# Odd layer: bias masked where it lands, and norm and stores between the products of the projection

## The reference, cut to what matters

```python
def natten_qkv(u, q_g, k_g):
    q, k, v = [t.reshape(B, T, NA_HEADS, NA_DIM) for t in jnp.split(u, 3, -1)]
    return rms_norm_2(q, q_g), rms_norm_2(k, k_g), v

def one_row(r):            # neighbourhood_attention, one row of 64 queries
    ...
    bias = jnp.transpose(rpb[:, drow][:, :, dcol], (0, 2, 1, 3))
    s_loc = einsum('bchd,bicjhd->bhcij', q_row, k_win) * scale + bias
    s_ctx = einsum('bchd,bnhd->bhcn', q_row, k_ctx) * scale
    p = softmax(concatenate([s_loc, s_ctx], -1))
    return p_loc @ v_win + p_ctx @ v_ctx
```

## Time and profile before

| | |
|---|---|
| runs of the kernel | 3016.82, 3017.26, 3021.13 us, median 3017.26 |
| span of the profiled execution | 3016.0 us |
| TensorE busy | 2677.4 us, 89% |
| VectorE busy | 1330.7 us, 44% |
| ScalarE busy | 490.4 us, 16% |
| GpSimd busy | 26.4 us, 1% |
| mean granted clock of TensorE | 0.955 |
| transfers | 651.34 MB, mean 216 GB/s |

### The profile page before, as it was taken

One profiled execution on the slowest core, in us unless ns is written; L12 is line 12 of the kernel. 1 busy time (PEld: TensorE's weight loads), 2 busy tenths in 40 slices (PEclk: granted clock), 3 DMA queues, 4 the chain that ended last, 5 costly groups with the idle time before them and its releaser, 6 DMA issues. The chain is left out here.

```text
span 3016.0 us, 44924 instructions
## 1 busy us (share of the span) xinstructions
PE 2677.4 (89%) x19748; PEld 1652.4 (55%) x19748; DVE 1330.7 (44%) x2509; ACT 490.4 (16%) x1158; POOL 26.4 (1%) x48
## 2 busy tenths in 40 slices
PE   7989999999999999998999989889979898865665
PEld 3467844446767888735753333345449687432323
DVE  2775488442473876586321111131367763100001
ACT  1023200000213000225221111020051311100000
POOL 0000000000000000000000000000000000000000
PEclk9999999999999999998999999999989999978878
DMA  9530255342352676220159999982110007899998
GB/s 358 195 140 26 87 195 223 139 168 112 112 195 71 251 279 248 75 84 29 59 232 402 427 428 428 427 339 46 44 36 30 2 25 301 366 427 428 427 427 353
DMA packets 67938, 651.34 MB, mean 216 GB/s; under 512 B 14880, under 2 KB 26912, under 8 KB 28064
## 3 DMA queue, kind: packets, MB, share of 16 engines
q1 hardware_dynamic: 67744, 648.47, 53.3%
HBM read 644.12 MB, written 4.33 MB: 215 GB/s over the span
## 5 line engine op out<-in xcount | busy, mean ns | idle before, releaser
L375 PE MATMUL ps<-HT,ring 128*128 128x256 f32 (+1 forms) x3152 | 901.3, 444 | 6.4 <-ACT HT L617 2.3
L375 PEld LDWEIGHTS ps<-HT,ring 128*128 128x128 f32 x3152 | 589.0, 190 | 284.5 <-issue 225.8
L2443 PE MATMUL ps<-ring,arena 128*32 128x256 f32 (+1 forms) x2944 | 372.9, 509 | 106.7 <-DMA ring<-in_moe_w 97.2
L477 DVE SCALAR_TENSOR_TENSOR acc<-ring,sil,acc 128x512 f32<-128x512 f32 x616 | 411.7, 744 | 0.0
L375 PE MATMUL ps<-arena,ring 128*128 128x256 f32 (+3 forms) x1232 | 373.6, 464 | 3.4 <-PEq L718 2.2
L2443 PEld LDWEIGHTS ps<-ring,arena 128*32 128x32 f32 (+1 forms) x2944 | 140.8, 131 | 315.0 <-issue 198.3
L375 PEld LDWEIGHTS ps<-arena,ring 128*128 128x128 f32 (+2 forms) x1232 | 230.1, 188 | 139.3 <-issue 119.3
L1042 DVE SCALAR_TENSOR_TENSOR XT<-ps,modcols,XT 128x256 f32<-128x256 f32 x124 | 55.7, 481 | 266.1 <-PE ps L375 140.4
L2464 PE MATMUL ps<-ring,arena 128*32 128x256 f32 x960 | 83.7, 510 | 58.6 <-DMA ring<-in_moe_w 58.6
L2464 PE MATMUL ps<-ring,conv 128*64 128x512 f32 x496 | 112.3, 596 | 24.0 <-DMA ring<-in_moe_w 23.3
L495 ACT ACTIVATE modrows<-ps 128x128 f32<-128x128 f32 x44 | 12.2, 278 | 574.8 <-PE ps L491 574.8
(11 more groups left out here) (431 smaller groups left out, 2611.4 us busy)
## 6 DMA issues: line engine op xcount, KB each, us to landing
ring<-in_moe_w SPq DMA_DIRECT2D x184, 2048.0 KB, 25.6
ring<-in_w_mod SPq DMA_DIRECT2D x24, 2048.0 KB, 8.1
ring<-in_ada_w SPq DMA_DIRECT2D x24, 2048.0 KB, 8.2
ring<-in_w_up SPq DMA_DIRECT2D x16, 2048.0 KB, 12.1
ring<-in_w_down SPq DMA_DIRECT2D x16, 2048.0 KB, 12.4
ring<-in_w_in SPq DMA_DIRECT2D x10, 2048.0 KB, 10.7
ring<-in_od_w_in SPq DMA_DIRECT2D x6, 2048.0 KB, 25.6
arena<-in_moe_w SPq DMA_DIRECT2D x10, 1024.0 KB, 20.4
```

The source lines that it names most:

```text
L375: last = nc.tensor.matmul(bank_of(job, j), lhsT, rhs, start=n == 0, stop=n == len(terms) - 1)
L477: ins = nc.vector.scalar_tensor_tensor(out=acc, in0=weights[:, k, :], scalar=s, in1=acc, op0=ALU.mult, op1=ALU.add)
L2443: last = nc.tensor.matmul(K.ps[M * j:M * j + M, 2 * (e % 2) + i, 0:FW], xs[:, e // 4 % 2, e % 4, 4 * h + k, :], weights((m, e, h), k, slic ...
```

## The change

Five things are edited, all in the odd layer. The queries are written with the tokens of each row in reverse (`by_row`), so that they match the order in which the bias lands; the mask table is reversed in the same way on the host, and the attention's outputs are copied out with rows turned back. The flip matrix is gone, and the mask is added in place by VectorE, one of eight parts ahead of each of jobs 19 to 26. The bias therefore stays where it lands, in `XT`'s context half and in `conv`. The norm of queries and keys is a class whose steps stand between jobs 12 and 21 of the projection. The two stores are seven, each sent as soon as its blocks have their taps. The clearing of the state moves to GpSimd's program inside the attention stage, where SP also waits for the stores before it starts its transfers.

```diff
@@ gemm_stage
                     K.load_next(sp)
+            if stores:
+                stores(sp)
             K.end_moves(sp, also)
@@ paired_attention_stage
+            if stored:
+                sp.wait_ge(*K.at("inputs_stored", 0))
             K.start_moves(sp, also)
             K.end_moves(sp, also)
+        @block.gpsimd
+        def _(pool):
+            if clear:
+                clear(pool)
...
-                    nc.vector.tensor_copy(pairs[j - 3]["out"], K.ps[:, 6 + (j - 3) % 2, 0:P]).then_inc(*K.inc("out_kept"))
+                    out, got = pairs[j - 3]["out"], K.ps[:, 6 + (j - 3) % 2, 0:P]
+                    if len(out.shape) == 3:
+                        got = got.rearrange("p (r t) -> p r t", t=GRID_W)
+                    nc.vector.tensor_copy(out, got).then_inc(*K.inc("out_kept"))
@@ odd_layer
+    def keep_reversed(b):
+        return lambda side, ps, act: nc.scalar.activation(by_row(q[:, b, :]), ps.rearrange("p (r t) -> p r t", t=GRID_W), ACT.Copy)
...
-    gemm_stage(K, 7, jobs, "odd_in_projection", feed=1, banks=SUMS, late=(1, also + position_bias(K, raw)), ...)
-    norm_stage(K, ...)
-    with K.block("masked_bias") as block:
...
-    K.end_stage()
+    bias = [XT[:, :, C], K.spare.rearrange("p (h n) -> p h n", h=8)]
+    window = K.constants(["window"], A[:, 14848:15360])
+    masked = MaskedBias(K, bias, len(window) + 32)
+    norm = QueryKeyNorm(K, q, k, A[:, 12800:13824], A[:, 15488:17536], A[:, 13824:14080], c)
+
+    def store_inputs(sp):
+        for b0, b1 in ((0, 4), (4, 8), (8, 12), (12, 15)):
+            sp.wait_ge(*evicted_by_vector(K, jobs, 11 + b1)())
+            sp.dma_start(K.u_dram[0]...[:, b0:b1], u[:, b0:b1, X]).then_inc(*K.inc("inputs_stored", 16))
+            if b0:
+                b1 = min(b1, 14)
+                sp.dma_start(K.u_dram[1]...[:, b0:b1], u[:, b0:b1, C]).then_inc(*K.inc("inputs_stored", 16))
+            if b0 == 4:
+                sp.wait_ge(*K.at("inputs_stored", 48))
+    gemm_stage(K, 7, jobs, "odd_in_projection", feed=1, banks=SUMS, late=(1, window + position_bias(K, bias)), stores=store_inputs,
+               steps=[((1, 6), c.sum_squares), ((2, 4), c.spread_root)] + norm.steps(14),
+               act_at=[(0, c.squares), (1, c.root_made), (3, c.biased)] + norm.act_at(12),
+               dve_at=[(0, c.gained), (0, c.fold_squares), (0, c.invert), (0, c.scaled)] + norm.dve_at(14) + masked.dve_at(19))
...
-    clear_recurrence(K, m)
     paired_attention_stage(..., stored=7, clear=lambda pool: clear_recurrence(K, m, pool))
+def by_row(a):
+    return a.rearrange("p (r t) -> p r t", t=GRID_W)[:, :, ::-1]
+class MaskedBias:
...
+    def add(self, dve, i):
+        if i == 0:
+            dve.wait_ge(*K.at("moved_aside", 16 * self.moves))
+        part = self.bias[i // 4][:, i % 4 * 2:i % 4 * 2 + 2, :]
+        K.nc.vector.tensor_tensor(part, part, self.window[:, i // 4, :].unsqueeze(1).broadcast_to([P, 2, T]), ALU.add)
+class QueryKeyNorm:
...
+    def add_up(self, pe):
+        pe.wait_ge(*self.context.at("row_made", 1))
+        for i, sq in enumerate(self.sq):
+            pe.wait_ge(*K.at("squares", i + 1))
+            for b in range(4):
+                for c in range(4):
+                    t = c * P % sq.shape[2]
+                    last = K.nc.tensor.matmul(K.ps[32 * c:32 * c + 32, SUMS, i * P:(i + 1) * P], K.pair_sums[:, 6 - 2 * b:38 - 2 * b],
+                                              sq[:, b, t:t + P], start=b == 0, stop=b == 3)
+    def spread(self, pe, i):
+        if i == 0:
+            pe.wait_ge(*K.at("inverted", 1))
+            pe.wait_ge(*self.context.at("chunk_scaled", KD))
+        elif i >= 2:
+            pe.wait_ge(*K.at("scaled", i - 1))
+        for n in range(4):
+            b, c = (2 * i + n // 2, n % 2) if i < 2 else (i - 2, n)
+            for h in range(2):
+                at = 32 * c + 2 * b + h
+                last = K.nc.tensor.matmul(K.ps[64 * h:64 * h + 64, self.bank(i), n * P:(n + 1) * P], K.ident[:, at:at + 1].broadcast_to([P, 64]),
+                                          self.root[:, (0 if i < 2 else P):(P if i < 2 else 2 * P)], start=True, stop=True)
...
+    def act_at(self, j):
+        return [(j, self.square), (j + 2, self.make_root)]
+    def steps(self, j):
+        return [((j, 0), self.add_up)] + [((j + 2 + i, 0), lambda pe, i=i: self.spread(pe, i)) for i in range(6)]
+    def dve_at(self, j):
+        return [(j + 1, self.invert)] + [(j + 2 + i, lambda dve, i=i: self.scale(dve, i)) for i in range(6)]
```

More of the change, by code:

```diff
@@ L300, in gemm_stage @@
 def gemm_stage(K, npieces, jobs, name="gemm", feed=None, also=(), before=None, ahead=None, banks=NBANK, steps=(), act_at=(), dve_at=(),
-               late=None, tail=None, early=(0, 0)):
+               late=None, tail=None, early=(0, 0), stores=None):
     nc, first = K.nc, K.cursor
@@ L939, in differential_attention_stage, with paired_attention_stage @@
     K.end_stage()
-def paired_attention_stage(K, pairs, work, name, also=()):
+def paired_attention_stage(K, pairs, work, name, also=(), stored=0, clear=None):
     nc, N = K.nc, len(pairs)
@@ L2604, in odd_layer @@
     v = A[:, 10752:12800].rearrange("p (t e) -> p t e", t=4)
-    jobs = [feature_job(K, 0, b * P, P, HT[:, :, X], q[:, b, :], only="act") for b in range(4)]
-    jobs += [feature_job(K, 1, b * P, P, HT, k[:, b, :]) for b in range(4)]
+    def keep_reversed(b):
+        return lambda side, ps, act: nc.scalar.activation(by_row(q[:, b, :]), ps.rearrange("p (r t) -> p r t", t=GRID_W), ACT.Copy)
+    jobs = [feature_job(K, 0, b * P, P, HT[:, :, X], None, only="act", evac=keep_reversed(b)) for b in range(4)]
@@ L2607, in odd_layer @@
+    jobs += [feature_job(K, 1, b * P, P, HT, k[:, b, :], only=("act", "dve")[b % 2]) for b in range(4)]
     jobs[4]["needs"] = lambda k: c.at("chunk_normed", k + 1)
-    jobs += [token_job(K, 2, lambda w, i: w[:, i, :], HT, t, v[:, t, :]) for t in range(4)]
+    jobs += [token_job(K, 2, lambda w, i: w[:, i, :], HT, t, v[:, t, :]) | dict(only=("act", "dve")[t % 2]) for t in range(4)]
     jobs += [shift_job(K, 3 + b // 4, b, HT[:, :, X] if b in LATENT_ONLY else HT, u[:, b, :]) for b in range(15)]
-    bias = HT[:, :, :].rearrange("p k t -> p (k t)").rearrange("p (c h n) -> p c h n", c=2, h=8)
@@ L2611, in odd_layer @@
[L2611 to L2622, removed]
@@ L2636, in odd_layer @@
-    K.end_stage()
+    bias = [XT[:, :, C], K.spare.rearrange("p (h n) -> p h n", h=8)]
[5 more added lines that the diff above has]
+            sp.wait_ge(*evicted_by_vector(K, jobs, 11 + b1)())
+            sp.dma_start(K.u_dram[0].rearrange("p (b t) -> p b t", b=15)[:, b0:b1], u[:, b0:b1, X]).then_inc(*K.inc("inputs_stored", 16))
+            if b0:
+                b1 = min(b1, 14)
+                sp.dma_start(K.u_dram[1].rearrange("p (b t) -> p b t", b=15)[:, b0:b1], u[:, b0:b1, C]).then_inc(*K.inc("inputs_stored", 16))
+            if b0 == 4:
+                sp.wait_ge(*K.at("inputs_stored", 48))
@@ L2637, in odd_layer @@
+    gemm_stage(K, 7, jobs, "odd_in_projection", feed=1, banks=SUMS, late=(1, window + position_bias(K, bias)), stores=store_inputs,
+               steps=[((1, 6), c.sum_squares), ((2, 4), c.spread_root)] + norm.steps(14),
+               act_at=[(0, c.squares), (1, c.root_made), (3, c.biased)] + norm.act_at(12),
+               dve_at=[(0, c.gained), (0, c.fold_squares), (0, c.invert), (0, c.scaled)] + norm.dve_at(14) + masked.dve_at(19))
     pairs = [dict(q=[q[64 * s:64 * s + 64, g, c * P:(c + 1) * P] for s in range(2)], k=[k[64 * s:64 * s + 64, g, :] for s in range(2)],
-                  v=[v[:, t, g * P:(g + 1) * P] for t in range(4)], bias=[bias[:, c, 2 * g + s, :] for s in range(2)],
@@ L2639, in odd_layer @@
-                  out=XT[:, g, T + c * P:T + (c + 1) * P])
+                  v=[v[:, t, g * P:(g + 1) * P] for t in range(4)], bias=[bias[c][:, 2 * g + s, :] for s in range(2)],
+                  out=by_row(XT[:, g, T + c * P:T + (c + 1) * P]))
              for g in range(4) for c in range(2)]
@@ L2662, in odd_layer, with __init__ @@
     experts(K, buffers, ahead, GroupNorm(K, m, buffers.B[:, 1860:1988]))
+def by_row(a):
+    return a.rearrange("p (r t) -> p r t", t=GRID_W)[:, :, ::-1]
+class MaskedBias:
+    def __init__(self, K, bias, moves):
+        self.K, self.bias, self.moves = K, bias, moves
+        self.window = K.const["window"].rearrange("p (c n) -> p c n", c=2)
+    def add(self, dve, i):
+        K = self.K
+        if i == 0:
[3 more added lines that the diff above has]
+    def dve_at(self, j):
+        return [(j + i, lambda dve, i=i: self.add(dve, i)) for i in range(8)]
@@ L2757, in rwkv_moves, with clear_recurrence @@
     return pairs + [(m.rkv, u[:, 0:3072]), (m.lg, u[:, 3584:3840])]
-def clear_recurrence(K, m):
+def clear_recurrence(K, m, pool):
     nc = K.nc
[L2764 to L2771, removed]
+    K.step(pool, nc.gpsimd.memset(m.state, 0.0), "cleared")
+    for low in m.low:
+        for d in range(2):
```

(4 more changed lines are left out.)

37 lines of the change are left out of this document (35 added, 2 removed).

## The result

The changed kernel took 3003.18 us (median of four runs, 3002.30 to 3008.96); the kernel before 3018.76 (median of the three runs in the table and one more). The ratio is 0.995, 95% interval 0.9937 to 0.9963: 15.6 us faster, where 18.4 were forecast and the range was 2995 to 3008. The profiled execution has 3000.9 us against 3016.0.

A forecast was written before the change was run, and what follows sets the result against it. The end was taken as bound by expert weight transfers that move one to one with the attention's start. Removing 28.05 us of stages and paying 9.6 gains 18.4: 3017.26 becomes 2998.9 us, range 2995 to 3008.

The forecast's parts named there:

- Step 1: Projection, ahead of product 14: 32 small products for sums of squares cost 2.05 us, upper end 3.4.
- Step 2: Projection, ahead of products 16 to 21: six spreads of eight products cost 5.91 us, between 3.1 and 7.9.
- Step 3: Projection: TensorE waits at spread 0 for VectorE's reciprocal, 0.2 us charged, between 0 and 1.75.
- Step 4: Projection: VectorE's six scalings and eight mask additions hide in its idle time, cost 0; without cover 10 us.
- Step 5: Projection's end: SP's last two store issues hold the stage, 1.1 us, between 0 and 2.53; their landing is hidden.
- step 6: Between projection and attention: one hand-over between stages, 0.34 us.
- Step 7: Attention: eight row-reversed copies cost 0, at worst 2.3 us; memsets beside its start cost 0, at worst 0.9.
- Step 8: Attention's start: TensorE's clock low as before, 0; if still high, 0.85 us gained; later nothing.
- Rival A: Projection: narrow products drop TensorE's clock once, losing 8.5 us; gain 9.9, 3007.4 us; chance 0.06.
- C: Projection: the low clock stays for its rest, from near product 14; 3078 us, slower than before; chance 0.03.
- B: Spreads run at the narrow rate and the attention starts at high clock: 5.9 us paid, 2995.1 us; chance 0.06.
- D: Behind the attention: the time saved is given back, the end doesn't follow; 3017 us if all; chance 0.03.

The follow-up runs named there:

- mask_only: Kernel before with only reversed queries and the mask added in place by VectorE, norm and clearing left as own stages: 3011.94 us (0.9974).
- sp_tail: Changed kernel with its last two stores issued by SP at the start of the attention instead of the projection's end: 3003.86 us, one run.
- busy_both: Changed kernel with unread constant products: three behind the projection's last product, three and two behind score products of attention pairs 1 and 2: 3008.75 us.
- clear_only: Kernel before with only the clearing of the recurrent state moved into GpSimd's program beside the attention: 3015.52 us (0.9991).
- spread_double: Changed kernel with each spread's eight products made twice, same result: 3004.68 us (0.9958).
- spread_four: Changed kernel with each spread's eight products made four times, same result: 3017.41 us (1.0).
- the second comparison: Changed kernel, unaltered, timed again in five rounds beside the kernel before (3019.26 us): 3002.53 us (0.9945).
- best: Changed kernel with last two stores issued in the attention, spreads in twos, and constant filler products behind the projection and in the attention: 3000.03 us (0.9938).
- kept_busy: Changed kernel with three unread constant products of 128x384 behind the projection's last product: 3002.28 us.

## Why the prediction was right

The sign, the place and the mechanism were right: 28.05 us went, and 28.05 - 17.22 = 10.8 was paid where the sum had 9.6.

- Step 1, the sums: 2.05 forecast. From the first tap of product 13 to that of 14, the changed kernel is 2.09 longer. Right; the row of the same form was the one to take. How much of the 2.09 is such a boundary as step 2 lacks, no run shows.
- Step 2, the spreads: the mis-sized term. 5.91 was forecast from 32 records in a row; 7.33 was paid, inside the bounds of 3.1 to 7.9. The rate was a little high (0.87 for eight products, where 0.98 was taken); what failed is that a price taken from a run of products was used for six separate groups, each with 0.35 us of boundary.
- Step 3, the wait at spread 0: 0.2 forecast, none found; the reciprocal ended 0.16 us ahead of it.
- Step 4, additions and scalings hidden: right (3.95 us of VectorE idle left in mask_only). In the changed kernel it is 3.95 ahead of product 22's taps, behind a mask addition, and 5.91 ahead of product 16's, behind a scaling, since each spread also puts the next product off. The first addition, at 2133.18, waited for no transfer.
- Step 5, SP's issues end the stage: right, and shown by sp_tail. With step 6, 1.44 was forecast and 1.42 measured. The stores' landing was hidden: SP waited 2.0 us for it and then, as before, for the attention to end, 23.7 us against 23.5. The waits of SP's queue in the changed kernel (waiter, what it waited for: us, times, longest):

```profile
SPq L953 <- PEq L953: 23.7, 1, 23.7
...
SPq L217 <- DMA rwkv_inputs<-arena: 2.0, 1, 2.0
```

- Step 7, reversed copies and memsets: 0, right (mask_only's 35.07 and busy_both's 34.12; clear_only's 0.43).
- Step 8, the clock at the attention's start: low, as forecast, and that is partly luck, since spread_double and spread_four started high after the same idle time. The price of a low start was right: 0.85 was taken, and clear_only's attention, high throughout, is 0.95 shorter than before. That nothing is lost later was wrong: the clock can fall again further in, and at 2202.75 VectorE waited 1.18 us for a score product. The forecast had 0 to 0.85 gained; the trace lost 1.26 in the attention, and another trace of the same kernel gained 0.8 on before. That 812.6 came out at 812.49 from the attention's start to the end is luck: from the memset behind the attention to the end it is 777.58 before and 776.16 after, and over the thirteen traces between 774.19 and 779.91.
- Rival A (a dip in the projection) fell: 91 us at 1.00 with seven steps in them. The swings between short idles that the Trainium skill tells of (TensorE: Matmul & The Clock Gate, "A second HAM failure mode: psum-queue depth-cycling") did not come: TensorE idled nowhere at these steps, so that the page's case was not met. C fell with it. B did not come in the profiled run: the spreads cost more than the narrow rate, and the attention started low. D fell by spread_four.

That leaves 18.4 - 17.2 = 1.2 us explained by step 2 (1.42 over, less the 0.2 of step 3). The rest, to the 15.6 of the medians, lies inside the runs' scatter: the second comparison gave 16.7. The time itself is 4.3 above the 2998.9 forecast: 2.8 by the gain, and 1.5 because the median of the kernel before had risen from 3017.26 to 3018.76. Product 26 ended 11.7 us later than before, where 8.2 were forecast: 9.4 by sums and spreads, and 2.28 by the unchanged part in front.

## What to carry to other kernels

Small products set into this dense stream of TensorE work did not bring the clock down, their inputs being ready, and cost their own time and a boundary (0.87 and 0.35 us for a spread): price each separate group with its boundary, and put groups together where their consumers allow. When a stage between two others goes away, look at what its neighbour's end now waits for: here two DMA issues on a queue, 1.1 us, which moved into the next stage without making it longer (best's attention took 34.10 us). Read a small change by the distance between two marks around it, since the unchanged code in front moved by more than most of the parts here.

## What was not expected of the hardware

The first tap of product 13, with the same TensorE work in front of it, moved over 7.5 us between traces (2094.76 to 2102.26).

The attention is 34.1 to 36.3 us long, with the same work. The three traces with a clock of 1.00 throughout (clear_only, busy_both, best) have 34.10 to 34.12, and every longer one has a low stretch in it; but kept_busy and spread_four have a low stretch of some 3 us and took 34.10 too, so that a low stretch costs only where it meets the path. What makes the clock fall, at the start or in the middle, is open: the two kernels with fillers in the attention, busy_both and best, stayed at 1.00, but so did clear_only without any, and spread_double and spread_four started high without any.
